# Gated linear unit of an S5 layer: seven half products from the third block on, in place of eight

## What is computed

```python
def ssm_layer(x, h0_re, h0_im, norm_pre, w_in, lam_re, lam_im, log_dt, b_re, b_im,
              c_re, c_im, d_skip, w_glu, b_glu, w_out, norm_post):
...
    ga, gb = jnp.split(jax.nn.gelu(y) @ w_glu + b_glu, 2, axis=-1)
    y = ga * jax.nn.sigmoid(gb) * jax.nn.silu(z)
    out = y @ w_out
    return x + rms_norm(out, norm_post), hr, hi
```

## Time and profile before

| what | us |
|---|---|
| median of 3 runs | 1414.78 |
| lowest and highest run | 1410.58, 1416.62 |
| the profiled execution, first to last instruction (span) | 1411.4 |
| TensorE busy in it | 1312.1 |
| VectorE busy | 676.0 |
| ScalarE busy | 484.0 |
| GpSimd busy | 483.8 |

### The profile page before, as it was taken

One profiled execution on the slowest core, in us unless ns is written; L12 is line 12 of the kernel. 1 busy time (PEld: TensorE's weight loads), 2 busy tenths in 40 slices (PEclk: granted clock), 3 DMA queues, 4 the chain that ended last, 5 costly groups with the idle time before them and its releaser, 6 DMA issues. The chain is left out here.

```text
span 1411.4 us, 28779 instructions
## 1 busy us (share of the span) xinstructions
PE 1312.1 (93%) x11781; PEld 1235.0 (88%) x11781; DVE 676.0 (48%) x1116; ACT 484.0 (34%) x833; POOL 483.8 (34%) x292
## 2 busy tenths in 40 slices
PE   4998879989889999999999999699999999898997
PEld 4888879989889999999999999599988888788785
DVE  5876678877811121212121100764238777576532
ACT  4223342326442222222222212333345555343531
POOL 2212210000024444444444344043357766665400
PEclk9999999999999999999999999899999999999999
DMA  8468884458533333333333325125255886675601
GB/s 198 91 118 133 141 144 117 134 172 286 207 78 113 104 97 104 98 104 105 105 108 97 90 81 128 31 75 170 77 171 152 275 264 190 225 268 153 237 16 46
DMA packets 248039, 194.22 MB, mean 138 GB/s; under 512 B 44753, under 2 KB 232041, under 8 KB 247185
## 3 DMA queue, kind: packets, MB, share of 16 engines
q1 hardware_dynamic: 247152, 159.48, 42.4%
q10 hardware_dynamic: 800, 33.53, 6.6%
HBM read 172.60 MB, written 53.87 MB: 160 GB/s over the span
## 5 line engine op out<-in xcount | busy, mean ns | idle before, releaser
L109 POOL TENSOR_TENSOR w_lo<-raw,w_hi 128x1024 fp32r<-128x1024 f32 x145 | 347.7, 2398 | 726.0 <-ACT w_hi L104 473.2
L167 PE MATMUL acc<-act_hi,w_hi 128*128 128x256 f32 x1728 | 352.5, 285 | 6.3 <-PEq L444 3.4
L167 PE MATMUL acc<-act_lo,w_hi 128*128 128x256 f32 x1728 | 350.8, 285 | 0.0
L167 PE MATMUL acc<-act_hi,w_lo 128*128 128x256 f32 x1728 | 350.2, 284 | 0.0
L167 PEld LDWEIGHTS acc<-act_hi,w_hi 128*128 128x128 f32 x1728 | 270.2, 190 | 8.7 <-issue 5.7
L167 PEld LDWEIGHTS acc<-act_hi,w_lo 128*128 128x128 f32 x1728 | 270.5, 190 | 0.0
L167 PEld LDWEIGHTS acc<-act_lo,w_hi 128*128 128x128 f32 x1728 | 270.4, 190 | 0.0
L104 ACT ACTIVATE w_hi<-raw 128x1024 fp32r<-128x1024 f32 x149 | 157.6, 1058 | 299.1 <-PE acc L167 256.1
L1399 DVE SCALAR_TENSOR_TENSOR sig<-acc,vec,sig 128x520 f32<-128x520 f32 x16 | 12.2, 760 | 289.6 <-PE acc L167 289.6
L2059 PE MATMUL acc<-act_hi,w_hi 128*128 128x256 f32 (+1 forms) x512 | 112.1, 301 | 12.2 <-ACTq L2379 11.7
L2059 PE MATMUL acc<-act_lo,w_hi 128*128 128x256 f32 (+1 forms) x512 | 104.3, 285 | 0.0
(11 more groups left out here) (324 smaller groups left out, 1936.1 us busy)
## 6 DMA issues: line engine op xcount, KB each, us to landing
raw<-a_w_glu SPq DMA_DIRECT2D x64, 512.0 KB, 4.0
s_kv<-cache_kv ACTq DMA_DIRECT2D x8, 4088.0 KB, 15.8
raw<-a_w_in SPq DMA_DIRECT2D x32, 512.0 KB, 4.3
raw<-b_w_in SPq DMA_DIRECT2D x32, 512.0 KB, 4.3
q_spread<-scratch_q SPq DMA_DIRECT2D x16, 768.0 KB, 7.1
raw<-a_w_out SPq DMA_DIRECT2D x16, 512.0 KB, 4.0
raw<-w_kv SPq DMA_DIRECT2D x16, 512.0 KB, 3.9
k_rows<-cache_kv SPq DMA_DIRECT2D x32, 256.0 KB, 5.2
```

The source lines that it names most:

```text
L109: pool.tensor_tensor(self.mem.wl[s][:, :, :], self.mem.raw[s][:, :, :], self.mem.wh[s][:, :, :].bitcast(F32), ALU.subtract).then_inc(self. ...
L167: ins = nc.tensor.matmul(mem.acc[a][:, 256 + lo:256 + hi], w[s][:, k, :], x[:, k0 + k, lo:hi], start=first and k == 0 and i == 0, stop=las ...
```

## The change

**What is multiplied.** The 520 columns and the 2048 rows of y are halved, and so are the weights of an output block: a and b (ga, gb) times the upper and lower 1024 rows (1, 2). That makes a 2 x 2 product of blocks, which takes eight half products. From block 2 on (`PLAIN = 2`, so 14 groups of one a and b each) Winograd's form with seven products is used. A product is 8 slices x 3 terms over 260 columns, 24 matmuls, all in one PSUM bank. Seven products are 168 matmuls, for 192.

**Sums of y** (t1 to t4), made once while the two plain blocks are multiplied: t1 to t3 in nine chunks on VectorE (`first_sum`, ScalarE's `sum_hi`, then three operations of `low_sum`, through PSUM), t4 on GpSimd in eight operations (`last_sum`) with ScalarE's `last_sum_hi`.

**Sums of weights**, four in each group, on VectorE through two PSUM pairs (`sum_weights`: 0 is gb1 + gb2, 1 is that less ga1, 2 is ga1 - gb1, 3 is ga2 less sum 1). ScalarE makes the high part of every weight block (`weights_hi`), VectorE the low part of the four sums (`sum_lo`), GpSimd that of the three plain ones (`raw_lo`, products 0, 1 and 6). Three slots take turns, and six raw buffers in place of two.

**Summands.** Products 0, 2, 4 and 6 go on in one bank that ScalarE moves out between them (`move_x`); products 1 and 5 and product 3 have a bank each, which VectorE adds (`move`). Two gates of 260 columns follow (`gate`, `store_y`), in a float copy of y; it is split into high and low parts only in the last group (`high`, `low`), four blocks at a time.

**Else.** The stage is written out without a loop; the semaphores of the stage before are cleared at its start; the next stages take their weight slots in exchanged order.

```diff
-    def __init__(self, nc, mem, name, units, first):
+    def __init__(self, nc, mem, name, units, first, slots=(0, 1)):
...
+        self.wh = [mem.wh[s] for s in slots]
...
+HALF_T = TOK // 2
+PLAIN = 2
+BLOCKS = ("ga1", "ga2", "gb1", "gb2")
+RAW_OF = {0: "ga1", 1: "ga2", 6: "gb2"}
+SUM_OF = {2: 1, 3: 0, 4: 2, 5: 3}
...
+    lo_half, hi_half = slice(0, HALF_T), slice(HALF_T, TOK)
+    chunks = [slice(0, 3), slice(3, 6), slice(6, 8)]
+    b11, b12 = ([x[:, 0:8, half] for x in (act_h, act_l)] for half in (lo_half, hi_half))
+    b21, b22 = ([x[:, 8:16, half] for x in (act_h, act_l)] for half in (lo_half, hi_half))
+    t1, t2, t3, t4 = ([th[j][:, :, :], tl[j][:, :, :]] for j in (1, 0, 2, 3))
+    y_sums = ((b12, b11, t1), (b22, t1, t2), (b22, b12, t3))
+    moving = (b11, b21, t2, t1, t3, b22, t4)
...
+    def block_at(g, name):
+        return (4 * g + BLOCKS.index(name) + 2) % 6
...
+    def bank_of(g, p):
+        return {1: y_bank, 5: y_bank, 3: z_bank}.get(p, x_bank[g % 2])
...
+        nc.clear_and_free_semaphores(mem.outputs_semaphores)
...
+            def load_block(g, name):
+                u, at = int(name[2]) - 1, (PLAIN + g) * P + (W2 if name[1] == "b" else 0)
...
+                if name == "gb2" and g >= 1:
+                    sp.wait_ge(summed, 4 * (g - 1) + 4)
+                    sp.wait_ge(w_lo, 3 * (g - 1) + 2)
...
+                sp.dma_start(raw[s][:, :, :], w[:, 8 * u:8 * u + 8, bass.ds(at, P)]).then_inc(raw_in[s], 16)
...
+                dn.load(sp, n, u, w[:, 8 * u:8 * u + 8, bass.ds((i + WT) * P - a * W2, P)])
+                if n == 5:
+                    sp.wait_ge(mem.states_stored, 64)
+                    for name in BLOCKS:
+                        load_block(0, name)
...
-            paired(pool, 3, 4 * WT, lambda n, q, h: dn.split_lo(pool, n, q))
+            def last_sum(c, step):
...
+                if step == 0:
+                    pool.wait_ge(y_sum_lo, 18)
+                    pool.tensor_tensor(x, b21[0][:, k, :].bitcast(F32), t2[0][:, k, :].bitcast(F32),
...
+                g, p = divmod(n, 7)
+                s = slot(n)
+                pool.wait_ge(w_hi, n + 1)
+                pool.tensor_tensor(wl[s][:, :, :], raw[block_at(g, RAW_OF[p])][:, :, :],
+                                   wh[s][:, :, :].bitcast(F32), ALU.subtract).then_inc(w_lo, 1)
...
+            for n in range(3, 6):
+                dn.split_lo(pool, n, n % 2)
+            raw_lo(0)
+            dn.split_lo(pool, 6, 0)
+            last_sum(0, 0)
+            dn.split_lo(pool, 7, 1)
+            for step in range(1, 4):
+                last_sum(0, step)
+            raw_lo(1)
+            for step in range(4):
+                last_sum(1, step)
+            for n in range(2, N):
+                if n % 7 in RAW_OF:
+                    raw_lo(n)
...
-            paired(pe, 1, 2 * WT, lambda m, a, h: dn.tile(pe, m, a, h, mem.acth, mem.actl))
+            for m in range(1, 2 * PLAIN):
+                dn.tile(pe, m, m % 2, m // 2, act_h, act_l)
+            for n in range(N):
+                g, p = divmod(n, 7)
...
+                if n == 0:
+                    pe.wait_ge(dn.acc_free[0], PLAIN + 1)
+                if n == 1:
+                    pe.wait_ge(dn.acc_free[1], PLAIN + 1)
+                if g == 0 and p in (2, 3, 4):
+                    pe.wait_ge(y_sum_lo, {3: 9, 2: 18, 4: 27}[p])
+                if g == 0 and p == 6:
+                    pe.wait_ge(p_sum_lo, 6)
+                if p == 0:
+                    if g >= 2:
+                        pe.wait_ge(x_moved, 4 * (g - 1))
+                elif p in (2, 4, 6):
+                    pe.wait_ge(x_moved, 4 * g + p // 2)
+                elif p == 1:
+                    pe.wait_ge(moved, 4 * g) if g else None
+                elif p == 3:
+                    pe.wait_ge(moved, 4 * (g - 1) + 3) if g else None
+                else:
+                    pe.wait_ge(moved, 4 * g + 1)
+                if p in RAW_OF:
+                    pe.wait_ge(w_lo, 3 * g + (0, 1, 6).index(p) + 1)
+                else:
+                    pe.wait_ge(w_lo_v, 4 * g + p - 1)
+                first, last = p in (0, 1, 3, 5), True
+                for k in range(8):
+                    for i, (a, x) in enumerate(((wh, xh), (wh, xl), (wl, xh))):
+                        ins = nc.tensor.matmul(bank_of(g, p), a[s][:, k, :], x[:, k, :],
+                                               start=first and k == 0 and i == 0, stop=k == 7 and i == 2,
+                                               skip_group_check=True)
+                ins.then_inc(multiplied, 1)
...
-            pe.wait_ge(dn.acc_free[0], WT + 1)
-            nxt.early_tile(pe, mem.yh, mem.yl, lambda k: pe.wait_ge(lo_r, k + 3))
...
-                if not first:
-                    dn.split_hi(act, 4 * i, 0, 2 * i)
-                    dn.split_hi(act, 4 * i + 1, 1, 2 * i)
-                    high(i - 1, 1 - s)
-                    dn.split_hi(act, 4 * i + 2, 0, 2 * i + 1)
...
+            def sum_hi(q):
+                act.wait_ge(y_sum, q + 1)
+                t, k = y_sums[q // 3][2], chunks[q % 3]
+                act.activation(t[0][:, k, :], chunk_in_psum(q), ACT.Copy).then_inc(y_sum_hi, 1)
...
+            def weights_hi(n):
+                g, p = divmod(n, 7)
...
+                if n >= 3:
+                    act.wait_ge(multiplied, n - 2)
+                elif n:
+                    act.wait_ge(dn.unit_read, 4 * PLAIN + n)
+                if p in RAW_OF:
...
+                    act.wait_ge(summed, 4 * g + max(SUM_OF[p] + 1, 2))
+                    src = e_bank[SUM_OF[p] % 2]
+                act.activation(wh[s][:, :, :], src, ACT.Copy).then_inc(w_hi, 1)
...
+            def move_x(n):
...
+                act.wait_ge(multiplied, n + 1)
...
+                if p == 0:
+                    act.wait_ge(gated, 2 * i)
+                    ins = act.activation(ga[:, lo_half], x, ACT.Identity, bias=b_a)
+                elif p == 2:
+                    ins = act.activation(ga[:, hi_half], x, ACT.Identity, bias=b_a)
+                elif p == 4:
...
+            def high(j, first, end):
+                act.wait_ge(gated, 2 * end)
...
+                        ins = act.activation(mem.yh[:, first:end, half], x[:, first:end, hi_half], ACT.Copy)
...
+            dn.split_hi(act, 3, 1, 1)
+            plain_sigmoid(0, ga)
+            for q in range(3):
+                sum_hi(q)
+            dn.split_hi(act, 4, 0, 2)
+            sum_hi(3)
+            sum_hi(4)
+            dn.split_hi(act, 5, 1, 2)
+            sum_hi(5)
+            weights_hi(0)
+            sum_hi(6)
+            dn.split_hi(act, 6, 0, 3)
+            sum_hi(7)
+            dn.split_hi(act, 7, 1, 3)
+            plain_sigmoid(1, gb)
+            last_sum_hi(0)
+            sum_hi(8)
+            weights_hi(1)
+            weights_hi(2)
+            for n in range(N):
+                g, p = divmod(n, 7)
+                if p in (0, 2, 4, 6):
+                    move_x(n)
+                if n + 3 < N:
+                    weights_hi(n + 3)
+                if n == 0:
+                    last_sum_hi(1)
+                if p == 5:
+                    sigmoid(g)
+                j = n - N + 5
+                if 0 <= j < 3:
+                    act.wait_ge(multiplied, n + 1)
+                    high(j, 4 * j, 4 * j + 4)
+                if n == N - 2:
+                    act.wait_ge(nxt.landed[0], 16)
+                    act.activation(nxt.wh[0][:, :, :], mem.raw[0][:, :, :], ACT.Copy).then_inc(nxt.hi_ready, 1)
+            act.wait_ge(nxt.landed[1], 16)
+            act.activation(nxt.wh[1][:, :, :], mem.raw[1][:, :, :], ACT.Copy).then_inc(nxt.hi_ready, 1)
+            high(3, 12, WT - 1)
+            high(4, WT - 1, WT)
...
-            def tile(i, s, h):
+            def first_sum(q):
+                a, b, _ = y_sums[q // 3]
...
+                if q >= 2:
+                    v.wait_ge(y_sum_lo, 3 * (q - 1))
+                v.tensor_tensor(chunk_in_psum(q), a[0][:, k, :].bitcast(F32), b[0][:, k, :].bitcast(F32),
+                                ALU.subtract).then_inc(y_sum, 1)
...
+            def low_sum(q):
...
+                v.wait_ge(y_sum_hi, q + 1)
+                v.tensor_tensor(x, x, t[0][:, k, :].bitcast(F32), ALU.subtract).then_inc(y_sum_lo, 1)
+                v.wait_ge(y_sum_lo, 3 * q + 1)
+                v.tensor_tensor(x, x, a[1][:, k, :].bitcast(F32), ALU.add).then_inc(y_sum_lo, 1)
+                v.wait_ge(y_sum_lo, 3 * q + 2)
+                v.tensor_tensor(t[1][:, k, :], x, b[1][:, k, :].bitcast(F32), ALU.subtract).then_inc(y_sum_lo, 1)
...
+                if i == 0:
+                    ins = v.tensor_tensor(e_bank[0], block("gb1"), block("gb2"), ALU.add)
+                elif i == 1:
+                    ins = v.tensor_tensor(e_bank[1], e_bank[0], block("ga1"), ALU.subtract)
+                elif i == 2:
```

(69 more changed lines are left out.)

245 lines of the change are left out of this document (181 added, 64 removed).

## The result

The changed kernel takes **1394.72 us** (median of 4, 1392.47 to 1400.61), the kernel before 1412.68 in the runs beside it (1410.48 to 1416.62): a ratio of **0.9883**, 95% interval 0.9853 to 0.9914. A repeat later gave 0.9872 (0.985 to 0.9894). That is 1.2% faster, by more than the measurement is uncertain. The forecast was 1403.

What follows compares the result with a forecast made beforehand. The prediction took TensorE's matmuls alone to bound the stage. Profiled 1411.4 - 40.4 removed + 16.2 start + 5.2 groups + 4.6 end + 2.5 clock = 1399.5, with the median 3.4 above: 1403 us, range 1384 to 1422.

Steps and rivals of the forecast that it cites:

- forecast case: Whole kernel: the predicted losses hold and the time lands at 1397 to 1408 us, chance 0.41.
- rival 1: Gated unit: VectorE's operations mostly fall between GpSimd's, so collisions miss; 1382 us, counted up to 1396, chance 0.27.
- Removed, 40.4 us: Groups from the third block on: 336 fewer matmuls at 0.1202 us each save 40.4 us.
- rival 4: Group products: chained writes to one bank slow each matmul; 10 ns gives back 23.5 us, 1427, chance 0.03.
- VectorE waits for GpSimd: Gated unit: a VectorE operation with two SBUF inputs waits for a running GpSimd operation, 2.8 us and not 0.70.
- Start, 16.2 us: Two plain blocks and first group: TensorE waits for late low parts, 16.2 us lost, 4.8 without collisions.
- the ring: Further groups: a loop of dependent steps beside TensorE takes 20.55 us, longer than TensorE's 20.19.
- Groups, 20.55 us, 5.2 in all: Further groups: TensorE loses 0.4 us in each of 13, given as 5 us, 5.2 in the sum.
- Loads do not add: Further groups: a block is asked for as the second sum ends and lands in 4.0 us, about when wanted.
- End, 4.6: Last group to output projection: product 7 waits 1.3 us, first output weights' low part 3.3 late, 4.6 in all.
- Clock, 2.5: TensorE after idle gaps: a clock fall costs about 3 us; 2.5 taken, between 0 and 6.
- Rival 3: Further groups: VectorE's loop bounds every group, 22.5 to 25 us each, 1428 to 1460 us, chance 0.15.

Runs made afterwards that it cites:

- e2_two_gates: The changed kernel with gate tile a doubled and used in turn by even and odd groups: 1397.11 us, ratio 0.9861 to the kernel before.
- e3_halves: The changed kernel with GpSimd's low part of each raw block of the groups done as two 512-column operations: 1395.25 us, ratio 0.9849 to the kernel before.
- e1_plain_first: The changed kernel with the start reordered, plain weights' high parts ahead of y-sum chunks on ScalarE: 1400.92 us, ratio 0.9885 to the kernel before.
- e8_end_order: The changed kernel with ScalarE converting the first output weights ahead of the third piece of y: 1397.39 us, ratio 0.9885 to the kernel before.
- e6_low_twice: The changed kernel with one added 768-column VectorE operation before product 3's low part, from the second group on: 1407.23 us, ratio 0.9959 to the kernel before.
- e4_no_last_sum: The changed kernel without the fourth y sum, product 6 taking an unsummed block instead: 1392.40 us, ratio 0.9841 to the kernel before.
- e5_fill_end: The changed kernel with 22 idle matmuls behind the last product, before the output projection: 1393.28 us, ratio 0.9863 to the kernel before.
- e11_end2: The changed kernel with first output weights earlier on ScalarE and y's low parts behind product 4 and 5 moves on VectorE: 1401.98 us, ratio 0.9888.

## Why the prediction was right

The time (1394.72, with 1403 forecast and 1384 to 1422 as range), the direction and most of the working held. The change was larger than forecast: 18.0 us against the kernel before beside it, 11.8 forecast. By the prediction's own bins the time does not lie in its forecast case (1397 to 1408) but in what it gave to rival 1 (up to 1396), whose condition was not met: the collisions did not mostly miss, there is one in each further group. Right mechanism, one term too large. Point by point:

- **Removed, 40.4 us**: 41.2. Matmuls of 260 columns into one bank are 119.8 ns apart, no slower than 120.2. So the chain in one bank (rival 4) costs nothing; e2_two_gates shows 2006 of them in 240 us without a break. The 110.8 ns by the Trainium skill's formula ("TensorE: Matmul & The Clock Gate", Back-to-back issue gap), which that section gives for one matmul by itself, are not reached here either.
- **VectorE waits for GpSimd**: shown, by e3_halves. It was the hidden price indeed: with halves the groups go from 20.55 to 20.25 us and the idle times at the end from 1.0 and 2.8 (before product 6 and before y) to 1.9 and 1.3, the last group with them from 24.9 to 23.7. For the first products it is only read from the rows (the first weight sum took 3.37 us); e3_halves left them as late as they were.
- **VectorE's price with PSUM**: forecast as for SBUF. The low part out of PSUM takes 1.22 us (L1703), the sum of two SBUF blocks 1.23 (L1695), writing to PSUM included. The 62 cycles more that the Trainium skill lists ("VectorE: DVE Perf Modes", the TRN2 errata) and its 1407 are not seen in this kernel.
- **Start, 16.2 us**: 14.7, half clock included. The gaps came at the forecast places (low parts 5 and 6, products 1 to 6) but were shorter: 2.61 and 2.19 for 3.2 and 4.1, product 3 idle 0 for 3.1. This is the term that was too large: less its half clock it is 9.7. TensorE idles 8.3 us between 433 and 490 (busy 48.67 of 57), half of the 16 that were to be the sign. And product 2 did not wait for a low part behind stores, as forecast, but for ScalarE's copy of product 0, which waited for the stores (2.07 us): the tile reuse of the ring, one group early. Its reasoning had a fault that the total hid. The walk added up the losses of the plain blocks and of the products, and e1_plain_first shows that the plain ones are worth nothing while the last y sum is behind: 8.4 us taken out, nothing won. The walk ran all queues forward in time, so its end was about right; what each of its losses is worth alone was not. (The losses it names add up to 16.3, where it says 16.2.)
- **Groups, 20.55 us, 5.2 in all**: 20.55, 5.6. The same ring. By the prediction's own figures the term is 13 x 0.36 = 4.7, not 5.2; TensorE's own turn was 20.12 and not 20.19, which made up for it. "Loads do not add" failed: the last block lands 0.9 to 1.6 us after VectorE is free for it, and where the sum then misses its place the group is 0.25 us longer. The walk let the sum in between the first two low parts of GpSimd in every group; groups of that form measure 20.4, so that 20.55 met the mean is luck to that extent.
- **End, 4.6**: 4.0 (1.2 at product 6, 2.79 before y). The forecast blamed the order on ScalarE; e8_end_order shows that VectorE's order stands right behind it.
- **Clock, 2.5**: 1.5 to 1.7 at the end, 1.6 behind product 2, and two falls in the plain blocks. Those were swallowed, as said: product 0 comes at 43.3 or 41.8, with the second fall or without, and product 1 at 46.8 in both. About 3.2 that count.
- **The 6.6 us between 1399.5 and the profiled 1392.9**: 2.5 from these terms (28.5 less 26.0), 0.8 from the pitch, and 3.3 are not in these terms: most of it lies outside the stage, which begins 0.9 earlier, with less time behind it. The begin of the stage varies by more than that from run to run (420.3 and 429.0), and the time from the first y product to the end by 1.6 (631.8 us in one run, 630.2 in the repeat), so nothing is read into them. The rest of the 8.3 us between 1403 and 1394.72: the forecast put the median 3.4 over the profiled execution, here it is 1.8.
- **Rival 3** (the loop becomes the bound): it is the bound already, by 0.4 us a group, but far from its 22 us. e6_low_twice bears out its price: 0.84 us more a group cost 10.8 us in the stage. The gain of 18 us would have been gone at 1.4 us more a group.

## What to carry to other kernels

When an algebraic saving moves work from TensorE to other engines, walk one turn of the loop as a ring of waits, tile reuse included: VectorE's share of 64% said nothing; with one shared tile the stage was 5 us longer than with two. Before mending a gap, ask what stands behind it on the slowest helper: 8.4 us of gaps and half clock were covered entirely by a later wait. Where VectorE must read two SBUF tiles beside GpSimd, cut GpSimd's operations in halves, or keep one operand in PSUM: of the changed kernel's 84 operations on 1024 columns with one input in PSUM and one in SBUF (L1693, L1697, L1703) none took over 1.23 us.

## What the runs showed that was not expected

TensorE's clock does not always fall after the same idle time. Behind 2.79 us at the end it falls in the changed kernel and in its repeat (37 matmuls in the 6 us behind at a granted clock of 0.72, pitch 0.22 us in part of them, the 1.2 GHz level, where 50 fit at 2.4 GHz), in e2_two_gates, e4_no_last_sum and e6_low_twice (2.78, 2.82 and 2.78 us idle, 37 or 38 matmuls), and not in e1_plain_first and e8_end_order (2.78 and 2.74 us idle, 50 matmuls). Behind the 2.6 us in the plain blocks it fell in all nine runs that have them. Behind the 2.2 us there it falls in five runs (the changed kernel, its repeat, e3_halves, e5_fill_end, e6_low_twice) and not in e2_two_gates, e4_no_last_sum, e8_end_order and e11_end2. A single run can so differ by 1.5 us for no reason of the edit; what decides it no run here shows.

VectorE and GpSimd take turns: while VectorE waits for a GpSimd operation, GpSimd's next one waits for VectorE in turn (up to 3.41 us in place of 2.39 at line 1488 of the changed kernel). Cutting a GpSimd operation in two costs it 0.17 us (twice 1.28 for 2.39).
